# Two latent projections interleaved tile by tile at the start of a decoder trunk, with their weight splits shared between GpSimd and ScalarE

## The reference

```python
h = rms_norm(x, norm_g)
z = h @ w_in                 # columns for three mixers and their gates
y_rnn = (rg_lru(x_rnn, ...) * silu(g_rnn)) @ rg_out
y_sc  = (sc_b * conv(sc_c * x_sc) * silu(g_sc)) @ sc_out
y_att = (mla(c_q, c_kv, k_rope, ...) * silu(g_att)) @ mla_out
gates = sigmoid(gate_logits + gate_b)
x = x + (gates[0]*y_rnn + gates[1]*y_sc + gates[2]*y_att) @ w_out
```

## Time and profile before

| what | value |
|---|---|
| median of 3 runs | 1712.31 us (1711.02 to 1712.64) |
| the profiled execution, its time | 1712.39 us |
| its span, first to last instruction | 1710.6 us |
| TensorE busy, matmuls | 1695.0 us, 99% of the span |
| GpSimd busy | 1204.9 us, 70% |
| VectorE busy | 893.9 us, 52% |
| ScalarE busy | 485.4 us, 28% |

### The profile page before, as it was taken

One profiled execution on the slowest core, in us unless ns is written; L12 is line 12 of the kernel. 1 busy time (PEld: TensorE's weight loads), 2 busy tenths in 40 slices (PEclk: granted clock), 3 DMA queues, 4 the chain that ended last, 5 costly groups with the idle time before them and its releaser, 6 DMA issues.

```text
span 1710.6 us, 32216 instructions
## 1 busy us (share of the span) xinstructions
PE 1695.0 (99%) x11928; PEld 1589.9 (93%) x11928; DVE 893.9 (52%) x1295; ACT 485.4 (28%) x867; POOL 1204.9 (70%) x1365
## 2 busy tenths in 40 slices
PE   7999999999999999999999999999999999999999
PEld 7999999999999999999999999999998888888887
DVE  7966758485545452212348757584856455322221
ACT  4423333332322331101125333333323313301110
POOL 7764848485688777777766748484857898777773
PEclk9999999999999999999999999999999999999999
DMA  4431222122232233222432313221322222323233
GB/s 156 139 102 62 92 72 81 66 92 85 89 108 76 86 114 109 86 96 88 159 120 76 110 58 97 65 90 64 93 91 93 98 86 86 143 92 98 90 120 113
DMA packets 49407, 164.21 MB, mean 96 GB/s; under 512 B 6048, under 2 KB 7456, under 8 KB 49056
## 3 DMA queue, kind: packets, MB, share of 16 engines
q1 hardware_dynamic: 41328, 146.56, 25.7%
q10 hardware_dynamic: 8032, 17.03, 3.0%
HBM read 152.21 MB, written 10.81 MB: 95 GB/s over the span
## 4 chain that ended last, share of the span: by engine, by line
PE 97%; DVE 2%; DMA 1%; ACT 0%; issue 0%; ACTq 0%; DVEq 0%
PE slots L508 85%; PE slots L573 3%; PE slots L606 2%; PE slots L668 2%; PE slots L591 1%; PE slots L542 1%; PE slots L558 1%; DMA residual_or_merged<-xt 1%; ACT residual_or_merged L956 0%; PE slots L576 0%; DVE branch_lo L1110 0%; DVE sc_acc L1395 0%; DVE sc_acc L1399 0%; PE slots L647 0%; DVE residual_or_merged L1348 0%
## 5 line engine op out<-in xcount | busy, mean ns | idle before, releaser
L420 POOL TENSOR_TENSOR w_lo<-w_raw,w_hi 128x256 fp32r<-128x256 f32 x1004 | 838.0, 866 | 20.9
L415 POOL TENSOR_SCALAR w_hi<-w_raw 128x1024 fp32r<-128x1024 f32 x251 | 291.1, 1160 | 334.6 <-PE slots L508 326.6
L508 PE MATMUL slots<-h_hi,w_hi 128*128 128x264 f32 (+1 forms) x2112 | 521.5, 311 | 0.0
L508 PE MATMUL slots<-h_lo,w_hi 128*128 128x264 f32 (+1 forms) x2112 | 515.4, 308 | 0.0
L508 PE MATMUL slots<-h_hi,w_lo 128*128 128x264 f32 (+1 forms) x2112 | 514.6, 308 | 0.0
L508 PEld LDWEIGHTS slots<-h_hi,w_hi 128*128 128x128 f32 x2112 | 342.7, 188 | 19.7
L508 PEld LDWEIGHTS slots<-h_hi,w_lo 128*128 128x128 f32 x2112 | 341.6, 188 | 19.1
L508 PEld LDWEIGHTS slots<-h_lo,w_hi 128*128 128x128 f32 x2112 | 342.0, 188 | 17.8
L508 PE MATMUL slots<-branch_hi,w_hi 128*128 128x264 f32 (+1 forms) x576 | 143.7, 313 | 11.3 <-DVE branch_lo L1110 9.4
L508 PE MATMUL slots<-branch_lo,w_hi 128*128 128x264 f32 (+1 forms) x576 | 142.4, 310 | 0.0
L508 PE MATMUL slots<-branch_hi,w_lo 128*128 128x264 f32 (+1 forms) x576 | 142.0, 310 | 0.0
(11 more groups left out here) (236 smaller groups left out, 2815.9 us busy)
## 6 DMA issues: line engine op xcount, KB each, us to landing
w_raw<-w_units SPq DMA_DIRECT2D x251, 512.0 KB, 3.3
stream<-sc_acc ACTq DMA_DIRECT2D x16, 264.0 KB, 2.1
sc_back<-stream SPq DMA_DIRECT2D x2, 2112.0 KB, 8.2
x_old<-stream SPq DMA_DIRECT2D x16, 264.0 KB, 4.4
stream<-residual_or_merged ACTq DMA_DIRECT2D x16, 264.0 KB, 2.4
ab_raw<-w_units SPq DMA_DIRECT2D x8, 512.0 KB, 4.2
residual_or_merged<-xt ACTq DMA_DIRECT2D x4, 528.0 KB, 8.1
stream<-xt ACTq DMA_DIRECT2D x1, 2112.0 KB, 10.2
```

Source lines behind the costliest of these rows:

```text
L415: pool.tensor_scalar(hi, raw, 1.0, 1.0, ALU.mult, ALU.mult).then_inc(sem("hi_part"), 1)
L420: op = pool.tensor_tensor(lo[:, cols], raw[:, cols], hi[:, cols].bitcast(F32), ALU.subtract)
L508: mm = pe.matmul(out[:, a_, 0:t1 - t0], w(k), x(k)[:, t0:t1], start=(n == 0), stop=(n == 3 * ks - 1))
```

## The change

At the start of layer 0, units 0 and 1 are worked on together. The staging buffers are both loaded in halves, in the order unit 0 first half, unit 1 first half, unit 0 second half, unit 1 second half. TensorE takes tile k of unit 0, then tile k of unit 1, for k from 0 to 7. Of the eight pieces of 256 columns, GpSimd makes the first hi piece; ScalarE makes the other seven (`first_upper`), put between its `x_upper` instructions; GpSimd makes all eight lo pieces. In both layers, ScalarE instead of VectorE writes the diagonals; for kv, the reciprocal comes before `h_whole(5)` instead of behind it. In layer 0 alone, the token sums of x come after five tiles of q0 instead of two, and the spread comes after two tiles of kr.

```diff
@@ SyncE
-                sp.dma_start(w_raw[0][:, 0:UNIT // 2], w_units[0, :, 0:UNIT // 2]).then_inc(sem("first_in"), 16)
-                sp.dma_start(w_raw[0][:, UNIT // 2:], w_units[0, :, UNIT // 2:]).then_inc(sem("unit_in0"), 16)
+                for half in range(2):
+                    cols = slice(half * (UNIT // 2), (half + 1) * (UNIT // 2))
+                    for u in range(2):
+                        sp.dma_start(w_raw[u][:, cols], w_units[u, :, cols]).then_inc(
+                            sem(f"unit_in{u}" if half else f"first_in{u}"), 16)
...
-                for j in range(l == 0, STAGES["CQ"][1]):
+                for j in range(2 * (l == 0), STAGES["CQ"][1]):
                     load("CQ", l, 0, j)
@@ GpSimd
+                for n in range(LO_PIECES):
+                    for u in range(2):
+                        if n == u == 0:
+                            pool.wait_ge(sem("first_in0"), 16)
+                            pool.tensor_scalar(first(w_hi, 0, 0), first(w_raw, 0, 0), 1.0, 1.0, ALU.mult,
+                                               ALU.mult).then_inc(sem("first_hi"), 1)
+                        pool.wait_ge(sem("first_hi"), 1) if n == u == 0 else pool.wait_ge(sem("next_hi"), 2 * n + u)
+                        pool.tensor_tensor(first(w_lo, u, n), first(w_raw, u, n), first(w_hi, u, n).bitcast(F32),
+                                           ALU.subtract).then_inc(
+                                               sem("first_split" if n < LO_PIECES - 1 else "unit_split"), 1)
@@ TensorE
+                def first_latents():
+
+                    outs = [free("CQ", l, 0, f"kv{u}") for u in range(2)]
+                    for k in range(KT):
+                        for u in range(2):
+                            if k < KT - 2:
+                                hi, lo = pieces_of(u)
+                                pe.wait_ge(sem("first_split"), k // 2 * 2 + u + 1)
+                            else:
+                                hi, lo = unit_ready("CQ", l, 0, u)
+                            pe.wait_ge(*at("xg_lo", l, 0, k + 1))
+                            mm = product(outs[u], hi, lo, tiles(xg_hi), tiles(xg_lo), KT, range(k, k + 1))
+                            if k == KT - 1:
+                                mm.then_inc(sem("unit_used"), 1)
...
+                ahead = 5 if l == 0 else 2
+                latent("q0", 2, range(0, ahead))
...
-                latent("q0", 2, range(2, KT))
+                latent("q0", 2, range(ahead, KT))
+                if l == 0:
+                    latent("kr", 3, range(0, 2))
                 out = free("NORM", l, 0, "spread")
                 spread(out, n_diag, lambda t: at("n_diag", l, 0, t + 1)).then_inc(sem("norm_mm"), 1)
-                latent("kr", 3)
+                latent("kr", 3, range(2 * (l == 0), KT))
@@ ScalarE
+            def diagonal(l, dst, values, signal):
+
+                lanes = TOK
+                for t, (t0, nt_) in enumerate(TOKS):
+                    act.activation(dst[0:lanes, t0:t0 + nt_], ident[0:lanes, 0:nt_], ACT.Identity, bias=zero[0:lanes],
+                                   scale=values[0:lanes, t:t + 1]).then_inc(sem(signal), 1)
...
+            def first_upper(u, n):
+
+                act.wait_ge(sem(f"unit_in{u}" if n >= LO_PIECES // 2 else f"first_in{u}"), 16)
+                act.activation(first(w_hi, u, n), first(w_raw, u, n), ACT.Copy).then_inc(sem("next_hi"), 1)
...
                 x_upper(0, k)
+                if k == 0:
+                    first_upper(1, 0)
+                elif k % 2 and k < KT - 1:
+                    for u in range(2):
+                        first_upper(u, k // 2 + 1)
...
+                act.wait_ge(*at("rinv", l, 0, 1))
+                diagonal(l, n_diag, k_inv, "n_diag")
                 q_latent(0)
...
+                act.wait_ge(*at("kv_rinv", l, 0, 1))
+                act.wait_ge(*ready("NORM", l, 0, "spread"))
+                diagonal(l, n_diag, q_sc, "kv_diag")
@@ VectorE
-                dve.wait_ge(*at("rinv", l, 0, 1))
-                diagonal(n_diag, k_inv, 0, "n_diag")
...
                 h_whole(4)
-                h_whole(5)
                 dve.wait_ge(*at("kv_rms", l, 0, 1))
                 dve.reciprocal(q_sc[:, 0:NTOK], q_ms[:, 0:NTOK]).then_inc(sem("kv_rinv"), 1)
-                dve.wait_ge(*at("kv_rinv", l, 0, 1))
-                diagonal(n_diag, q_sc, 0, "kv_diag")
+                h_whole(5)
```

More of the change, by code:

```diff
@@ L320, in tile, with first @@
             return buf[:, bass.ds(c, 1), :].rearrange("p a t -> p (a t)")
+        def first(buf, u, n):
+            return buf[u][:, n * (UNIT // LO_PIECES):(n + 1) * (UNIT // LO_PIECES)]
         block = ctx.enter_context(nc.Block())
@@ L431, in split_first @@
             def split_first():
-                width = UNIT // LO_PIECES
                 for n in range(LO_PIECES):
[L435 to L444, removed]
+                    for u in range(2):
[7 more added lines that the diff above has]
+                                               sem("first_split" if n < LO_PIECES - 1 else "unit_split"), 1)
             for l in range(DEPTH):
@@ L448, in _ @@
                     split_first()
-                for j in range(l == 0, 6):
+                for j in range(2 * (l == 0), 6):
                     split_unit("CQ", l, 0, j)
@@ L522, in dense @@
                 out = free(stage, l, i, name)
-                first = stage == "CQ" and l == j == 0
-                hi, lo = (pieces_of(0) if first else unit_ready(stage, l, i, j))
+                hi, lo = unit_ready(stage, l, i, j)
                 for k in ks:
[L526 to L529, removed]
                     if tile_there:
@@ L618, in latent @@
                     dense("CQ", l, 0, name, j, xg_hi, xg_lo, lambda k: at("xg_lo", l, 0, k + 1), False, ks)
-                latent("kv0", 0)
-                latent("kv1", 1)
-                latent("q0", 2, range(0, 2))
+                def first_latents():
[12 more added lines that the diff above has]
+                if l == 0:
+                    first_latents()
+                else:
+                    latent("kv0", 0)
+                    latent("kv1", 1)
+                ahead = 5 if l == 0 else 2
+                latent("q0", 2, range(0, ahead))
                 if l == 0:
@@ L852, in _ @@
                 roots("NORM", l, 0, "stat", k_ms, D, "n_rms")
+                if l == 0:
+                    act.wait_ge(sem("params_in"), 48)
+                act.wait_ge(*at("rinv", l, 0, 1))
+                diagonal(l, n_diag, k_inv, "n_diag")
                 q_latent(0)
@@ L1098, in lo_part @@
                 dve.tensor_tensor(dst, full, hi.bitcast(F32), ALU.subtract).then_inc(sem(signal), 1)
[L1100 to L1105, removed]
             def x_lower(l, c):
```

## The result

The change made the kernel slower, where no change or a gain of 2 us was forecast. The median of 14 executions is 1716.37 us (1714.21 to 1716.91), against 1712.47 us (1709.35 to 1713.04) for the kernel before in 14 executions taken beside them: a ratio of 1.0024, 95% interval 1.0018 to 1.0031. The profiled execution took 1715.93 us with a span of 1714.1 us, 3.5 us more than the 1710.6 of before. One execution of a later experiment, at 2055.98 us and a mean granted clock of 0.751 where all others lie between 0.995 and 0.999, is left out of every comparison.

The account below looks back on a forecast made before the run. TensorE, busy 99% of the span, was taken as the bound, so only its waits could yield. Gains of 1.7 (unit 2) and 0.43 us (norm), 2.1 in all, gave 1710.2 us, range 1708.2 to 1712.5.

Parts of the forecast that it names:

- the 0.43 us: Layer 0 norm: the wait for the diagonal at the spread goes; gain 0.43 us, bounds 0 and 0.43.
- rival A: The forecast itself: unit 2 is late by about 2 us, time 1710.2 us; chance 0.45.
- Rival C: Unit 2's split: each VectorE addition blocks GpSimd for its whole 0.69 us, q0 at 25.0, time 1711.3 us; chance 0.2.
- near the sum of both engines' work alone: Shared port of VectorE and GpSimd: each one's contended instruction, 1.14 and 1.26 us, said to be near this sum.
- slower first stretch: Kernel before, TensorE's first tiles: three tiles took 3.74 us where 2.19 would do.
- Unit 2: The deciding term: load lands at 17.9, split takes 5.9 us, q0 starts at 23.9; gain 1.7 us, bounds 3.7 and 0.
- The gain of 3.7 for the two units: TensorE, units 0 and 1: their 16 tiles end at 21.9 us, 3.7 before the present 25.60.
- TensorE waits 2 us: Ahead of q0: TensorE idles from 21.9 until unit 2 is split, with q0 at 23.9.
- Afterwards: Step for everything after layer 0's norm: unit 3 in time, kv diagonal costs ScalarE 1.8 us under cover, layer 1 gains 0.
- It has q1's eight tiles, 5.85 us, as cover: Both layers: `h_upper(4)` and `h_lower(4)`, waiting behind ScalarE's 1.8 us kv diagonal, are covered by q1's tiles.
- Rival E: TensorE comes early to kv's spread or attention and waits for VectorE's h chain: 1712.3 us; chance 0.1.
- that the sums come later costs nothing: Layer 0 norm: later token sums cost 0, since the adding ends at about 23 us.

Follow-up runs that it names:

- the last experiment: Changed kernel with covered TensorE waits dropped and layer 0's old order of sums and spread, no halves, kv diagonal on ScalarE: 1711.69 us, ratio 1.0006.
- the padded kernel: Kernel before, with 17 waits already met put ahead of q0 on TensorE and nothing else changed: 1714.9 us, ratio 1.0019.
- the trimmed one: Changed kernel with 12 already covered wait instructions fewer on TensorE: 1712.08 us, ratio 0.9999 to the kernel before.
- the clock experiment: Changed kernel with 22 useless matmuls between units 1 and 2, so TensorE works through its wait: 1712.56 us, ratio 1.0006.
- the version with halves and the changed order: Changed kernel with units 2 and 3 loaded and split in halves and covered waits dropped, diagonals on ScalarE: 1711.31 us, ratio 0.9998.
- the version with all repairs: Changed kernel with units 2 and 3 in halves, covered waits dropped, kv diagonal on VectorE, old order around layer 0's spread: 1708.38 us, ratio 0.9984.

## Why the prediction was wrong, by its own steps

**What held.** The first matmul came at 8.77 (forecast 8.68), the end of the 16 tiles at 22.13 (21.9) with no wait inside, the 128x256 copy took 0.42 us (0.41), the five diagonals 1.94 (1.8), GpSimd idled for 2.24 us for w_raw ("two microseconds"), and the spread needed no wait (the 0.43 us were gained). The mechanism of rival A, that unit 2 is late because its staging buffer comes free late, was right, and so was its cause in the additions of VectorE: cutting five of them saved 1.63 us of the split. The price of one was near as well: about 0.4 us, for 0.43. Rival C charged a whole addition, 0.69, and that was too much, although the rows above agree with engines that take turns. The prediction's "near the sum of both engines' work alone" was loose: 0.72 + 0.69 = 1.41, and the rows have 1.14 and 1.26. Its "slower first stretch" had another cause than the split: there, too, a pair of matmuls takes 0.64 us up to 11.02, and 0.41 from 12.17 on.

**Unit 2: a term mis-sized by 1.2 us.** q0 started at 25.09, not 23.9. The copy at 12.04 stood waiting for unit 1's second half, issued near 2.6 us and taken to land near 10.5; it landed at 12.0. So unit 0's split ended near 15.5 and not 14.7, and unit 2's pieces began at 18.91 and not 17.9. The rest is 0.2 us more of split. The gain of 3.7 for the two units was left at 0.5; rival C's 25.0 was the nearest, by another road. The trap: the last of four transfers was given the landing time of one with the same place but another neighbour.

**"TensorE waits 2 us" was priced as time alone.** Five tiles behind the wait took 5.41 us at a granted clock of 0.57, and 3.88 with the engine kept at work: 1.53 us that the sum had no term for. The kernel before had an idle of 1.88 us at 19.48 with the clock at 1.00 behind it, so the row nearest at hand spoke for no charge; the wait turned out 2.96. But before's own trace has falls, one in each layer at attention's entry, behind matmuls of one column and with no idle at all. In layer 0:

```profile
54.49 1.95 PE slots L647 x20
```

```profile
57.00:61.00 4.00, 4.00 (x26) 4.00 (x25) 3.10 (x6) 1.56 (x3) 3.92 (x5) 0.66 0.91 328
```

So a charge for the clock was there to be seen. The Trainium skill (TensorE: Matmul & The Clock Gate, Why this matters for your kernels) names gaps of idle time on TensorE as what throws it back to the lower clock. This trace agrees after 2.96 us; behind 2.24 us in the last experiment's profile there is no fall, and behind 1.88 us there is one in the padded kernel and none in the kernel before.

**A step that the prediction didn't have: TensorE's own instructions.** "Afterwards" costed edits by engine time alone. The 9 more wait instructions ahead of attention's loop made 2.05 us of stall on entering it. That waits alone do this is shown both ways, by the padded kernel before (+2.65 us from q2's start to the values) and the trimmed one. The row of the stall is the loop's entry branch, 3.27 us where all kernels without the stall have 0.32. That it waits for the loop's code is read from the transfer of the code queue that lies within it; no row ties the two together. It fits a rule of the Trainium skill (Runtime: NRT & Kernel Launch, Instruction fetch mechanics), by which a taken branch to code that isn't in the fetched pages waits for a DMA of it. The traces agree in that the time is spent at a branch with a fetch in it. With the loop moved still further (the clock experiment) the stall goes although there are 30 fetches, which that rule allows.

**"It has q1's eight tiles, 5.85 us, as cover ... Layer 1 ... so 0."** Wrong in both layers. The spread was covered, but not the chain behind it: h_upper(4), h_lower, cq_lo, the copies, up to the copy that frees attention's slot. VectorE's timeline of the kernel before in layer 1 has that copy as

```profile
915.26 0.70 DVE L1215 COPY residual_or_merged<-slots 128x528 f32<-128x528 f32 x1
```

so it ended at 915.96, only 0.28 us ahead of the values at 916.24. The move of the diagonal makes VectorE's chain later, and TensorE came out 0.37 us late in that stretch and waited 0.24 in layer 0. Taking it back set layer 1 right.

**Rival E** ("TensorE waits there for VectorE's h chain") had chance 0.1. Its mechanism is what limits the version with halves and the changed order (2.9 us, together with the kv diagonal). Whether "that the sums come later costs nothing" holds once TensorE is early, no run shows alone: the version with all repairs took the sums earlier and waited 0.8 us for them.

The sum against the span: forecast -2.1, measured +3.5, 5.6 apart. Unit 2 gives 1.2, the clock 1.5, the entry stall 2.05, VectorE's lateness at the entry 0.24, what comes between layer 0's values and layer 1's 0.52: 5.5. Removing the stall by fewer waits lowered the median by 4.3 us and not 2. The other 2.3 go with the clock: at the same mean granted clock the two kernels differ by 2.1 and 1.9 us. Why the clock is low for less time in some executions, and in more of them without the stall, stays open.

## What to carry to other kernels

Read slack at the last semaphore of a chain (here the copy that frees a slot for attention), not at the nearest consumer, before calling a moved instruction covered. A wait of TensorE can cost more than its length (2.96 us cost 1.53 more here), and extra waits on an engine that enters an aligned loop can cost too although each is free: look at the loop's entry branch in the view of its source line, and drop repeated waits. Where two units are worked on at once, free their staging by halves. That alone broke even here (0.9998), and so did the norm's old order alone (1.0006); with both and the kv diagonal back on VectorE the kernel gained (0.9984), and which of the last two it takes is not separated. Compare small changes at the same mean granted clock.

## What the hardware showed that I had not expected

- 17 waits already met, added to TensorE's stream, cost 2.65 us at one loop's entry; 12 wait instructions fewer than the change has took 1.84 us away there. The chain shows the lost time as "issue" or under a wrong releaser. The loop's entry branch shows it: 3.27 to 3.79 us in the four kernels that stall, 0.32 in the six others.
- An idle of 2.96 us on TensorE was followed by some 3 us at the lower clock (0.57 granted between 25 and 29 us). An idle of 1.88 us was followed by none in the kernel before and by a fall in the padded one (0.65 from 21 to 25 us), one of 2.24 us by none, and twenty matmuls of one column by a fall without any idle in the kernel before (0.66 from 57 to 61 us), and by none in the last experiment's profile (1.00 in the same stretch).
- The times of one kernel go by the mean granted clock of the execution: 1710.17 us at 0.999, 1711.63 at 0.998 and 1712.94 at 0.997 for the kernel before.
- Four transfers of 256 KB issued within 1.5 us landed with the last one 9.4 us after its issue, where 6.4 to 8.4 us were seen before.
- VectorE's additions beside GpSimd's split lengthened it from 4.45 to 6.08 us, about 0.4 us for each of four; GpSimd's 128x256 subtraction took 1.13 us on average beside them and 0.83 with five of seven cut. An addition of 8 columns took 0.17 us alone and 0.97 beside GpSimd, ending with GpSimd's instruction.
